# Attention's second product with its operands exchanged: the values stay in TensorE, the turned weights stream, and the division comes ahead of the turn

## The chip, the cores and the metric

The kernel runs on one core of one Trainium2 chip. The metric is the device time of one execution in microseconds, the median of several runs.

## The reference

Two transformer-like blocks are computed in fp32 on a sequence of 256 tokens of width 1024. The first block has two layers, and each layer holds a feed-forward network, a mixer and a second feed-forward network. Half of the mixer is a state-space part, the other half is an attention with 16 heads of width 64; both halves go through one output projection. The attention is a sum of three dilated causal windows whose softmax denominators are joined, which is the same as one softmax with a count for each pair of query and key. What matters here, cut down:

```python
for i in range(DEPTH):                       # 2 layers
    x = x + 0.5 * swiglu(rms_norm(x, ffn1_norm[i]), ...)
    z, xbc, dt_raw, q, k, v = split(rms_norm(x, mix_norm[i]) @ w_in[i])
    y_ssd = ssd_mixer(...)                   # (256, 1024)
    q, k = rms_norm(q, q_norm[i]), rms_norm(k, k_norm[i])
    # per head: p = exp(scores - m); den = sum(p); o = (p / den) @ v
    y_att = dilated_attention(q, k, v)       # (256, 1024)
    x = x + concatenate([y_ssd, y_att]) @ w_out[i]     # w_out: 2048 x 1024
    x = x + 0.5 * swiglu(rms_norm(x, ffn2_norm[i]), ...)
```

The second block (gated linear attention, a convolution branch, 32 experts) follows and is not touched.

## The kernel before

TensorE's order is written out by hand, and so is that of VectorE (`dve`) and ScalarE (`act`). The engines meet at semaphores. Four banks of PSUM (`misc`) are handed round: the fill with number m uses bank m % 4, TensorE waits in `claim_bank` until the fill four numbers earlier has been drained (`drained[m % 4]`), and `attention_fills()` numbers the fills of the attention: `S` for a head's scores, `T` for its turned weights and then its values, `Y` for a turn of the attended rows.

The attention of a layer is a loop over 19 steps, h = 0 to 18. It is a pipeline over heads, and the output projection is laid between its pieces:

- TensorE in step h: `scores(h)` (four instructions, lines 1211 and 1212; a plain fp32 product is two instructions), `turn_weights(h-2)` (three transposes, L1218), in steps 7, 11 and 15 also `turn_values` (four transposes, L837), `values(h-3)` (L1225), and then as many halves of rows of the output projection as `HALVES[h]` says (`out_rows`). A half is 12 instructions of 128 by 256, lines 815 to 817: the fp32 product is made of three fp32r ones, of high and low parts. The first two rows, in steps 0 and 1, are plain fp32 (L1248).
- VectorE in step h: `maxima(h)` (L2869, L2871, L2876: mask added, maximum, its scaled negative), `attended(h-3)` (L2881 the reciprocal of the sum, L2884 the values times it, from PSUM into `yatt`), in the same three steps `values_low` (L2859, low part of the turned rows), and `out_low_piece` (L2849, the low part of a row of `w_out`).
- ScalarE in step h: the exponentials of head h in two pieces with their sums (L2130, L2132), the copy of the turned weights of head h-2 out of PSUM into `pT` (L2141), `out_high_piece` (L2115, the high part of a row of `w_out`), and `values_turned` (L2124, the high part of the turned rows).

In `values(h)` a head's turned weights are the loaded (stationary) operand, and 64 columns of v stream: three products, six instructions. The result has queries on partitions. It is scaled into `yatt`, and four times per layer 256 columns of `yatt` are turned so that the output projection finds features on partitions. After step 18 come the last `turn_values(3)`, the last half of row 13, `modulation` (L1301) and rows 14 and 15; then the second feed-forward network starts (L887).

Of the kernel before, what the change touches and what calls it, by code (L numbers as in the profile page):

```python
# [116 lines left out]
def attention_fills():  # L117

    order = []
    for h in range(HEADS + 2):  # L120
        if h < HEADS:
            order.append(("S", h))
        if h >= 2:
            order.append(("T", h - 2))
        if h in TURNS:
            order.append(("Y", TURNS[h]))
    order.append(("Y", 3))
    return {step: i for i, step in enumerate(order)}


TURNS = {7: 0, 11: 1, 15: 2}
HALVES = (2, 2, 1, 2, 1, 2, 1, 1, 2, 1, 2, 1, 2, 1, 2, 1, 2, 1, 0)
PLAIN = 2
OUT_HOME = (0, None, 2, 0, None, 2, 0, None)
# [4 lines left out]
def two_blocks(nc, d, out):  # L139
    fills = []  # L140
    slots, rows_d = [], []
    for l in range(DEPTH):
        fills += [(("mod", 2), 1), (("mod", 3), 1)] * l + [(("norm", 3 * l), 4)] * (not l)
        fills += [(("ffn", 2 * l), NF)] + [("params", 4)] * (not l)
        fills += [(("mod", 4 * l), 1)]
        fills += [(("xbc", l), 8), (("dt", l), 1), (("z", l, 0), 1), (("xt", l), 4), (("bt", l), 1),
                  (("z", l, 1), 1), (("z", l, 2), 1), (("acum", l), 1), (("z", l, 3), 1), (("cb", l), 2)]
        for j in range(8):
            fills += [(("qk", l, j), 1), (("bc", l, j), 1)]
        fills += [(("v", l, 0), 1), (("v", l, 1), 1), (("state", l), 2), (("v", l, 2), 1), (("off", l), 2),  # L150
                  (("v", l, 3), 1), (("qkt", l), 8), (("yt", l), 4), (("att", l), 2 * HEADS + 4),
                  (("mod", 4 * l + 1), 1), (("ffn", 2 * l + 1), NF)]
        slots += [(("ffn", 2 * l), NF), (("win", l), 24), (("wout", l), 8), (("ffn", 2 * l + 1), NF)]
        rows_d += [(("ffn", 2 * l), NF), (("ffn", 2 * l + 1), NF)]
# [18 lines left out]
    with ctx:  # L173
# [293 lines left out]
        ysd_ready = sem("ysd_ready")  # L467
        smax_ready = sem("smax_ready")
        p_exp = sem("p_exp")
        av_done = sem("av_done")  # L470
        pt_ready = sem("pt_ready")
        out_done = sem("out_done")
# [198 lines left out]
        def y_low_of(k):  # L671

            first_ = Y_LOW + (1 - k // KD) * SLOT + k % KD * SEQ
            return high_b[:, :, :].rearrange("p a b -> p (a b)")[:, first_:first_ + SEQ]

        def turned_q(k):

# [134 lines left out]
        def _(pe):  # L812
# [391 lines left out]
            def attention_and_out(l, a):  # L1204
# [7 lines left out]
                    pe.matmul(b[:, P:3 * P], q[:, P:SEQ], k, start=True, stop=True).then_inc(filled, 1)  # L1212

                def turn_weights(h):
                    pe.wait_ge(p_exp, HEADS * l + h + 1)
                    b = claim_bank(m0 + AF["T", h])
                    for c in range(3):
                        mm = pe.transpose(b[:, c * P:(c + 1) * P], sp3[:, h % 3, c * P:(c + 1) * P], ident)  # L1218
                    mm.then_inc(filled, 1)

                def values(h):
                    pe.wait_ge(pt_ready, HEADS * l + h + 1)
                    b = bank_of(m0 + AF["T", h])
                    for t, c, key in ((0, 0, 0), (1, 1, 0), (1, 2, 1)):
                        mm = pe.matmul(b[:, 3 * P + t * HD:3 * P + (t + 1) * HD], pT[:, h % 2, c * P:(c + 1) * P],  # L1225
                                       v[:, key, h * HD:(h + 1) * HD], start=(key == 0), stop=(key == t),
                                       skip_group_check=True)
                    mm.then_inc(av_done, 1)

                def turn_values(q):  # L1230
                    for h in range(4 * q, 4 * q + 4):
                        wait_drained(pe, m0 + AF["T", h])
                    turn(m0 + AF["Y", q] - q, yatt, [q])

                def row_in(k):
                    wait_drained(pe, m0 + AF["Y", (k - KD) // 2] if k >= KD else FILL["yt", l] + k // 2)
                    if k < PLAIN:
                        wait_slot(n0 + k // 2)
                    else:
                        pe.wait_ge(out_low_in, (2 * KD - PLAIN) * l + k - PLAIN + 1)  # L1240
# [27 lines left out]
                for h in range(HEADS + 3):  # L1268
                    if h < HEADS:
                        scores(h)  # L1270
                    if 2 <= h < HEADS + 2:
                        turn_weights(h - 2)
                    if h in TURNS:
                        turn_values(TURNS[h])
                    if h >= 3:
                        values(h - 3)
                    if h == 0:
                        pe.wait_ge(acc_free, a)
                    for k, c in itertools.islice(rows_left, HALVES[h]):
                        mm = out_rows(k, c)  # L1280
                        if k % 2 and c:
                            mm.then_inc(freed[(n0 + k // 2) % SLOTS], 1)
                turn_values(3)
                for k, c in rows_left:
                    out_rows(k, c).then_inc(freed[(n0 + k // 2) % SLOTS], 1)
                modulation(4 * l + 1)
# [532 lines left out]
        def _(act):  # L1819
# [297 lines left out]
            def attention(l):  # L2117
                m0 = FILL["att", l]
                scale = HD ** -0.5

                def values_turned(q):
                    m = m0 + AF["Y", q]
                    wait_filled(act, m)
                    act.activation(xl[:, 2 * q:2 * q + 2, :], bank_of(m).rearrange("p (a b) -> p a b", a=2),  # L2124
                                   ACT.Copy).then_inc(y_high, 1)

                for h in range(HEADS + 2):
# [7 lines left out]
                    if h >= 2:  # L2135
                        hh = h - 2
                        m = m0 + AF["T", hh]
                        wait_filled(act, m)
                        if hh >= 2:
                            act.wait_ge(av_done, HEADS * l + hh - 1)  # L2140
                        act.activation(pT[:, hh % 2, :], bank_of(m)[:, 0:3 * P], ACT.Copy).then_inc(pt_ready, 1)  # L2141
                    if h in HIGH_AT:
                        out_high_piece(l, HIGH_AT[h])
                    if h in TURNS:
                        values_turned(TURNS[h])
                values_turned(3)

            def evac(m, n, dst, src_n, func=ACT.Copy, scale=1.0):

# [288 lines left out]
        def _(dve):  # L2438
# [413 lines left out]
            def attention(l):  # L2852
                m0 = FILL["att", l]

                def values_low(q):
                    dve.wait_ge(y_high, 7 * l + 3 + q + 1)
                    m = m0 + AF["Y", q]
                    first_ = Y_LOW + 2 * q * SEQ
                    dve.tensor_tensor(high_b[:, :, :].rearrange("p a b -> p (a b)")[:, first_:first_ + 2 * SEQ], bank_of(m),  # L2859
                                      xl[:, 2 * q:2 * q + 2, :].rearrange("p a b -> p (a b)").bitcast(F32), ALU.subtract)\  # L2860
                        .then_inc(drained[m % 4], 1)

                def maxima(h):
                    m = m0 + AF["S", h]
# [11 lines left out]
                    dve.tensor_scalar(nmx[:, 2 * h:2 * h + 2], mx[:, 2 * h:2 * h + 2], -(HD ** -0.5), None,  # L2876
                                      ALU.mult).then_inc(smax_ready, 1)

                def attended(h):
                    dve.wait_ge(p_exp, HEADS * l + h + 1)  # L2880
                    link(dve.reciprocal(rden[:, 2 * h:2 * h + 2], den[:, 2 * h:2 * h + 2]))  # L2881
                    dve.wait_ge(av_done, HEADS * l + h + 1)
                    m = m0 + AF["T", h]
                    dve.tensor_tensor(yatt[:, :, h * HD:(h + 1) * HD],  # L2884
                                      bank_of(m)[:, 3 * P:4 * P].rearrange("p (t e) -> p t e", t=NT),
                                      rden[:, 2 * h:2 * h + 2].unsqueeze(2).to_broadcast([P, NT, HD]), ALU.mult)\
                        .then_inc(drained[m % 4], 1)

                for h in range(HEADS + 3):
                    if h < HEADS:  # L2890
                        maxima(h)
                    if h >= 3:
                        attended(h - 3)
                    if h in TURNS:
                        values_low(TURNS[h])
                    if h in LOW_AT:
                        out_low_piece(l, LOW_AT[h])
                values_low(3)

            def modulation(p):  # L2900
                m = FILL["mod", p]
# [526 lines left out]
            for l in range(DEPTH):  # L3428
# [10 lines left out]
                    modulation(0)  # L3439
                ssd_and_projections(l)  # L3440
                for q in range(1, 4):
                    dve.wait_ge(y_high, 7 * l + q)
# [71 lines left out]
```

## Time and profile before

| what | value |
|---|---|
| median of 3 runs | 2089.66 us (2089.42 to 2098.31) |
| profiled execution, its own time | 2090.49 us |
| its span, first to last instruction | 2088.6 us |
| attention loop, layer 0 | 368.05 to 436.05 us |
| attention loop, layer 1 | 987.63 to 1055.64 us |

The loop is counted from the first instruction of `scores(0)` to the first instruction of the half row that follows the last `turn_values`. Both layers take 68.0 us, 136 us of the span together. Durations of TensorE instructions overlap, because matmuls are pipelined: what one of them costs is the distance from its start to the start of the next.

### The profile page before, as it was taken

The page shows a single profiled execution, that of the slowest core. Times are in us where ns is not written, and L with a number is a line of the kernel's source. Part 1 is how long each engine was busy: PE and PEld are TensorE (multiplying, and loading weights), DVE is VectorE, ACT ScalarE, POOL GpSimd, SP SyncE. Part 2 cuts the span into 40 slices and gives each one's busy share as a digit, 9 for nine tenths or more (in the row PEclk, how much of TensorE's full clock was granted, in tenths as well). Part 3 has the DMA queues.
Part 4 walks back from the last instruction along what each step waited for, and adds up shares of the span by engine and source line. Part 5 has one row for each costly group of instructions (what it writes and reads, how often), then busy time and mean ns, then how long its engine had stood idle before and what let it go on. Part 6 is the DMA issues. An engine that isn't in the chain of part 4 may idle for free. (4 is left out here: it accounts for less than half of the span.)

```text
span 2088.6 us, 37979 instructions
## 1 busy us (share of the span) xinstructions
PE 2049.4 (98%) x14933; PEld 1896.7 (91%) x14933; DVE 1689.3 (81%) x2097; ACT 1224.8 (59%) x1537; POOL 472.4 (23%) x253
## 2 busy tenths in 40 slices
PE   8999999999999999999999999999999999999997
PEld 8999999999999999999999998999877777777775
DVE  5887868667777877868677756998689999999998
ACT  5435565653335335666653335444378888888886
POOL 4894000008932981000009900000000000000000
PEclk9999999999999999999999999999999999999999
DMA  8875554257766774554247853445569999999994
GB/s 252 282 257 175 168 158 160 82 172 247 256 212 201 252 253 160 164 162 139 102 164 262 272 176 104 134 134 192 217 250 373 365 372 368 373 366 374 364 369 182
DMA packets 238942, 483.74 MB, mean 232 GB/s; under 512 B 10613, under 2 KB 178977, under 8 KB 222465
## 3 DMA queue, kind: packets, MB, share of 16 engines
q1 hardware_dynamic: 226880, 443.58, 60.6%
q0 software_dynamic: 11360, 37.21, 5.4%
q10 hardware_dynamic: 608, 1.65, 0.2%
q8 instruction: 65, 1.06, 0.2%
q14 instruction: 29, 0.23, 0.0%
HBM read 481.31 MB, written 1.09 MB: 231 GB/s over the span
## 5 line engine op out<-in xcount | busy, mean ns | idle before, releaser
L816 PE MATMUL misc<-xhl,ring_low 128*128 128x256 f32 x1568 | 436.5, 278 | 0.0
L815 PE MATMUL misc<-xhl,high_b 128*128 128x256 f32 x1376 | 384.1, 279 | 1.0 <-ACT xnT L1951 1.0
L817 PE MATMUL misc<-xhl,high_b 128*128 128x256 f32 x1376 | 382.8, 278 | 0.0
L816 PEld LDWEIGHTS misc<-xhl,ring_low 128*128 128x128 f32 x1568 | 295.0, 188 | 0.8
L3258 DVE TENSOR_TENSOR ring_low<-ring,high_b 128x2048 fp32r<-128x2048 f32 x128 | 287.1, 2285 | 0.6 <-issue 0.6
L2526 DVE TENSOR_TENSOR ring_low<-ring,high_b 128x2048 fp32r<-128x2048 f32 x92 | 262.8, 2894 | 10.1 <-ACT high_b L1894 9.7
L815 PEld LDWEIGHTS misc<-xhl,high_b 128*128 128x128 f32 x1376 | 260.0, 189 | 2.3 <-ACT xnT L1951 1.2
L817 PEld LDWEIGHTS misc<-xhl,high_b 128*128 128x128 f32 x1376 | 258.6, 188 | 0.0
L2253 ACT ACTIVATE high_b<-ring 128x2048 fp32r<-128x2048 f32 x124 | 235.7, 1914 | 33.7 <-DMA ring<-in_w_dram 33.2
L1794 POOL TENSOR_SCALAR arena<-arena,cact 128x1024 f32<-128x1024 f32 x56 | 213.0, 3803 | 4.9 <-DMA arena<-in_w_ada_dram 1.9
L1926 ACT ACTIVATE misc<-arena 128x256 f32<-128x256 f32 x66 | 25.7, 389 | 309.0 <-DVE arena L2574 309.0
L1550 PE MATMUL misc<-high_b,u_rows 128*128 128x512 f32 x512 | 204.1, 399 | 1.9 <-DVE u_rows L3301 1.2
L1552 PE MATMUL misc<-ring_low,u_rows 128*128 128x512 f32 x512 | 199.9, 391 | 0.0
L1894 ACT ACTIVATE high_b<-ring 128x2048 fp32r<-128x2048 f32 x92 | 170.9, 1904 | 3.1 <-DMA ring<-in_ffn_w_up_dram 3.1
L1791 POOL TENSOR_SCALAR arena<-arena,cact 128x1024 f32<-128x1024 f32 x4 | 14.5, 3618 | 615.8 <-DVE hidhl L2553 607.9
L815 PE MATMUL acc<-hidhl,high_r 128*128 128x256 f32 x528 | 148.3, 281 | 0.9 <-DVE ring_d_low L2532 0.7
L3264 DVE TENSOR_TENSOR ring_d_low<-ring_d,high_r 128x1024 fp32r<-128x1024 f32 x128 | 147.9, 1215 | 0.5
L817 PE MATMUL acc<-hidhl,high_r 128*128 128x256 f32 x528 | 147.3, 279 | 0.0
L816 PE MATMUL acc<-hidhl,ring_d_low 128*128 128x256 f32 x528 | 147.3, 279 | 0.0
L815 PE MATMUL misc<-ring_low,xhl 128*128 128x256 f32 x512 | 145.2, 284 | 1.7 <-DVE arena L2746 1.7
L2258 ACT ACTIVATE high_r<-ring_d 128x1024 fp32r<-128x1024 f32 x128 | 129.2, 1052 | 9.1 <-DMA ring_d<-in_w_dram 8.5
L1550 PEld LDWEIGHTS misc<-high_b,u_rows 128*128 128x128 f32 x512 | 96.0, 188 | 35.5 <-DVE ring_low L3258 11.0
(492 smaller groups left out, 5556.9 us busy)
## 6 DMA issues: line engine op xcount, KB each, us to landing
ring<-in_w_dram SPq DMA_DIRECT2D x128, 1024.0 KB, 7.8
ring<-in_w_in_dram SPq DMA_DIRECT2D x72, 1024.0 KB, 5.4
ring_d<-in_w_dram SPq DMA_DIRECT2D x128, 512.0 KB, 4.8
ring<-in_ffn_w_gate_dram SPq DMA_DIRECT2D x44, 1024.0 KB, 5.4
ring<-in_ffn_w_up_dram SPq DMA_DIRECT2D x44, 1024.0 KB, 9.1
ring_d<-in_ffn_w_down_dram SPq DMA_DIRECT2D x88, 512.0 KB, 7.2
arena<-in_w_ada_dram POOLq DMA_DIRECT2D x48, 512.0 KB, 5.1
ring<-in_w_out_dram SPq DMA_DIRECT2D x20, 1024.0 KB, 4.9
```

The costliest lines, as they stand in the source:

```text
L815: pe.matmul(dst, wh, ml, start=start, stop=False, **kw)
L816: pe.matmul(dst, wl, mh, start=False, stop=False, **kw)
L817: return pe.matmul(dst, wh, mh, start=False, stop=stop, **kw)
L1550: pe.matmul(b, ue[:, k, half, :], expert_part(high_b, x)[:, kk, :], start=(k == 0), stop=False)
L1552: mm = pe.matmul(b, ue[:, k, half, :], expert_part(ring_low, x)[:, kk, :], start=False, stop=(k == KD - 1))
L1794: pool.tensor_scalar(row, row, cact[:, k:k + 1], None, ALU.mult).then_inc(pool_step, 1)
L1894: act.activation(high_b[:, s, :], ring[:, s, :], ACT.Copy).then_inc(high_in[s], 1)
L2253: act.activation(high_b[:, s, :], ring[:, s, :], ACT.Copy).then_inc(high_in[s], 1)
L2258: act.activation(high_r[:, s, :], ring_d[:, s, :], ACT.Copy).then_inc(high_in_d[s], 1)
L2526: dve.tensor_tensor(ring_low[:, s, :], ring[:, s, :], high_b[:, s, :].bitcast(F32), ALU.subtract)\
L3258: dve.tensor_tensor(ring_low[:, s, :], ring[:, s, :], high_b[:, s, :].bitcast(F32), ALU.subtract)\
L3264: dve.tensor_tensor(ring_d_low[:, s, :], ring_d[:, s, :], high_r[:, s, :].bitcast(F32), ALU.subtract).then_inc(low_in_d[s], 1)
```

## The change

`values(h)` is written the other way round: 128 columns of v (the pair of heads that h belongs to) are loaded and the head's turned weights stream, 256 columns for the first 128 keys and 128 columns for the second. The result has features on partitions, and only the 64 partitions of head h are used. It lands in columns 0 to 255 of the head's own `T` bank, where the turned weights were. Because queries are now along the free axis, the division by the sum is made earlier: VectorE's `weighted(h-1)` in step h takes the reciprocal and multiplies the weights in place (128 and 256 columns), and `turn_weights` waits for it (`p_scaled`) and no longer for the exponentials. `yatt` and its turns are gone. The high and low parts are now made for each head, on 64 partitions of 256 columns: ScalarE's `values_out(h-3)` at the end of step h, ahead of `out_high_piece`, and VectorE's `values_low(h-3)`, which waits for it, ahead of `out_low_piece`. The `T` bank is drained by `values_low`. Rows 8 to 15 of the output projection wait for their two heads' banks.

```diff
-        if h in TURNS:
-            order.append(("Y", TURNS[h]))
-    order.append(("Y", 3))
...
                 def turn_weights(h):
-                    pe.wait_ge(p_exp, HEADS * l + h + 1)
+                    pe.wait_ge(p_scaled, HEADS * l + h + 1)
...
                 def values(h):
                     pe.wait_ge(pt_ready, HEADS * l + h + 1)
                     b = bank_of(m0 + AF["T", h])
-                    for t, c, key in ((0, 0, 0), (1, 1, 0), (1, 2, 1)):
-                        mm = pe.matmul(b[:, 3 * P + t * HD:3 * P + (t + 1) * HD], pT[:, h % 2, c * P:(c + 1) * P],
-                                       v[:, key, h * HD:(h + 1) * HD], start=(key == 0), stop=(key == t),
-                                       skip_group_check=True)
-                    mm.then_inc(av_done, 1)
-                def turn_values(q):
-                    for h in range(4 * q, 4 * q + 4):
-                        wait_drained(pe, m0 + AF["T", h])
-                    turn(m0 + AF["Y", q] - q, yatt, [q])
+                    ks = slice(h // 2 * P, (h // 2 + 1) * P)
+                    pe.matmul(b[:, 0:SEQ], v[:, 0, ks], pT[:, h % 2, 0:SEQ], start=True, stop=False, skip_group_check=True)
+                    pe.matmul(b[:, P:SEQ], v[:, 1, ks], pT[:, h % 2, SEQ:3 * P], start=False, stop=True,
+                              skip_group_check=True).then_inc(av_done, 1)
...
                 def row_in(k):
-                    wait_drained(pe, m0 + AF["Y", (k - KD) // 2] if k >= KD else FILL["yt", l] + k // 2)
+                    if k < KD:
+                        wait_drained(pe, FILL["yt", l] + k // 2)
+                    else:
+                        for h in range(2 * (k - KD), 2 * (k - KD) + 2):
+                            wait_drained(pe, m0 + AF["T", h])
...
-                if h in TURNS:
-                    turn_values(TURNS[h])
-                turn_values(3)
...
-                def values_turned(q):
-                    wait_filled(act, m)
-                    act.activation(xl[:, 2 * q:2 * q + 2, :], bank_of(m).rearrange("p (a b) -> p a b", a=2),
+                def values_out(h):
+                    act.wait_ge(av_done, HEADS * l + h + 1)
+                    act.activation(y_high_of(KD + h // 2)[half_of(h), :], bank_of(m0 + AF["T", h])[half_of(h), 0:SEQ],
                                    ACT.Copy).then_inc(y_high, 1)
...
                         act.activation(pT[:, hh % 2, :], bank_of(m)[:, 0:3 * P], ACT.Copy).then_inc(pt_ready, 1)
+                    if h >= 3:
+                        values_out(h - 3)
                     if h in HIGH_AT:
                         out_high_piece(l, HIGH_AT[h])
-                    if h in TURNS:
-                        values_turned(TURNS[h])
...
+                def values_low(h):
+                    dve.wait_ge(y_high, 19 * l + 3 + h + 1)
+                    m = m0 + AF["T", h]
+                    k = KD + h // 2
+                    dve.tensor_tensor(y_low_of(k)[half_of(h), :], bank_of(m)[half_of(h), 0:SEQ],
+                                      y_high_of(k)[half_of(h), :].bitcast(F32), ALU.subtract).then_inc(drained[m % 4], 1)
...
-                def attended(h):
+                def weighted(h):
                     dve.wait_ge(p_exp, HEADS * l + h + 1)
                     link(dve.reciprocal(rden[:, 2 * h:2 * h + 2], den[:, 2 * h:2 * h + 2]))
-                    dve.wait_ge(av_done, HEADS * l + h + 1)
-                    m = m0 + AF["T", h]
-                    dve.tensor_tensor(yatt[:, :, h * HD:(h + 1) * HD], ...
+                    for t, cs in ((0, slice(0, P)), (1, slice(P, 3 * P))):
+                        ins = dve.tensor_scalar(sp3[:, h % 3, cs], sp3[:, h % 3, cs], rden[:, 2 * h + t:2 * h + t + 1],
+                                                None, ALU.mult)
+                    ins.then_inc(p_scaled, 1)
...
                     if h < HEADS:
                         maxima(h)
+                    if 1 <= h <= HEADS:
+                        weighted(h - 1)
                     if h >= 3:
-                        attended(h - 3)
-                    if h in TURNS:
-                        values_low(TURNS[h])
+                        values_low(h - 3)
                     if h in LOW_AT:
                         out_low_piece(l, LOW_AT[h])
-                values_low(3)
```

## Rows read from the trace of the kernel before

**Rows 1.** The page: busy time of each engine over the span.
```profile
PE 2049.4 (98%) x14933; PEld 1896.7 (91%) x14933; DVE 1689.3 (81%) x2097; ACT 1224.8 (59%) x1537; POOL 472.4 (23%) x253
```

**Rows 2.** Busy time of each engine by stretch, attention loop of layer 0.
```profile
core 0: us, PE busy (x) PEld busy (x) DVE busy (x) ACT busy (x) POOL busy (x), PEclk, DMA share, GB/s
378.70:428.00 49.30, 49.30 (x412) 48.00 (x410) 29.27 (x105) 31.15 (x83) 0.00 (x0) 1.00 0.29 105
428.00:436.10 8.10, 7.45 (x67) 7.34 (x65) 2.91 (x8) 1.05 (x3) 0.00 (x0) 1.00 0.75 259
```

**Rows 3.** Waits between 366 and 440 us, longest first.
```profile
engine line waited for: us in total, times, longest us
ACT arena L2130 <- DVE arena L2876: 21.1, 14, 3.1
DVE arena L2869 <- PE misc L1212: 15.9, 12, 2.1
```

**Rows 4.** Timeline of TensorE, starts of steps 3, 4 and 9 to 10.
```profile
378.67 0.39 PE L1211 MATMUL misc<-arena 128*128 128x128 f32 x2
...
383.17 0.39 PE L1211 MATMUL misc<-arena 128*128 128x128 f32 x2
...
401.57 0.38 PE L1211 MATMUL misc<-arena 128*128 128x128 f32 x2
401.79 0.60 PE L1212 MATMUL misc<-arena 128*128 128x256 f32 x2
402.22 0.49 PE L1218 MATMUL misc<-konst,arena 128*128 128x128 f32 x3
402.55 0.78 PE L1225 MATMUL misc<-arena 128*128 128x64 f32 x6
403.14 0.37 PE L815 MATMUL acc<-high_b,ring_d_low 128*128 128x256 f32 x1
...
404.60 0.38 PE L1211 MATMUL misc<-arena 128*128 128x128 f32 x2
```

**Rows 5.** Timeline of TensorE, the end of the loop.
```profile
428.00 0.49 PE L1218 MATMUL misc<-konst,arena 128*128 128x128 f32 x3
...
434.24 0.78 PE L1225 MATMUL misc<-arena 128*128 128x64 f32 x6
435.67 0.63 PE L837 MATMUL misc<-konst,arena 128*128 128x128 f32 x4 [0.66 <-DVE arena L2884]
436.05 0.36 PE L815 MATMUL acc<-high_b,ring_d_low 128*128 128x256 f32 x1
```

**Rows 6.** Timeline of VectorE, around steps 8 and 9.
```profile
398.24 0.69 DVE L2859 TENSOR_TENSOR high_b<-misc,xhl 128x512 fp32r<-128x512 f32 x1 [1.97 <-ACT xhl L2124]
398.85 1.22 DVE L2849 TENSOR_TENSOR ring_low<-ring,in_z 128x1024 fp32r<-128x1024 f32 x1
399.98 0.28 DVE L2869 CUSTOM_DVE_ANT_0 arena<-misc,konst 128x128 f32<-128x128 f32 x1
...
402.43 0.29 DVE L2869 CUSTOM_DVE_ANT_0 arena<-misc,konst 128x128 f32<-128x128 f32 x1
...
435.12 0.29 DVE L2884 TENSOR_TENSOR arena<-misc,arena 128x128 f32<-128x128 f32 x1 [1.72 <-PE misc L1225]
```

**Rows 7.** Timeline of ScalarE, around steps 7 and 9.
```profile
397.63 0.58 ACT L2124 ACTIVATE xhl<-misc 128x512 fp32r<-128x512 f32 x1
...
403.31 0.40 ACT L2130 ACTIVATE arena<-arena 128x128 f32<-128x128 f32 x1
...
404.20 0.47 ACT L2141 ACTIVATE arena<-misc 128x384 f32<-128x384 f32 x1
404.57 1.04 ACT L2115 ACTIVATE ring_d_low<-ring 128x1024 fp32r<-128x1024 f32 x1
```

**Rows 8.** Groups by line and shape: busy us, mean ns | idle before.
```profile
L3301 DVE TENSOR_TENSOR u_rows<-misc,u_rows 128x256 fp32r<-128x256 f32 x68 | 25.7, 415 | 3.5 <-ACT u_rows L2290 3.4
L2290 ACT ACTIVATE u_rows<-misc 128x256 fp32r<-128x256 f32 x68 | 24.2, 378 | 22.1 <-PE misc L1538 22.1
L2998 DVE TENSOR_SCALAR arena<-arena,colc,colb 128x256 f32<-128x256 f32 x4 | 1.4, 408 | 0.2 <-DVE arena L3015 0.2
```

More of the change, by code:

```diff
@@ L124, in attention_fills @@
             order.append(("T", h - 2))
-        if h in TURNS:
-            order.append(("Y", TURNS[h]))
-    order.append(("Y", 3))
     return {step: i for i, step in enumerate(order)}
-TURNS = {7: 0, 11: 1, 15: 2}
 HALVES = (2, 2, 1, 2, 1, 2, 1, 1, 2, 1, 2, 1, 2, 1, 2, 1, 2, 1, 0)
@@ L150, in two_blocks @@
         fills += [(("v", l, 0), 1), (("v", l, 1), 1), (("state", l), 2), (("v", l, 2), 1), (("off", l), 2),
-                  (("v", l, 3), 1), (("qkt", l), 8), (("yt", l), 4), (("att", l), 2 * HEADS + 4),
+                  (("v", l, 3), 1), (("qkt", l), 8), (("yt", l), 4), (("att", l), 2 * HEADS),
                   (("mod", 4 * l + 1), 1), (("ffn", 2 * l + 1), NF)]
@@ L469, in two_blocks @@
         p_exp = sem("p_exp")
+        p_scaled = sem("p_scaled")
         av_done = sem("av_done")
@@ L674, in y_low_of, with half_of @@
             return high_b[:, :, :].rearrange("p a b -> p (a b)")[:, first_:first_ + SEQ]
+        def half_of(h):
+            return slice(h % 2 * HD, (h % 2 + 1) * HD)
         def turned_q(k):
@@ L2119, in attention @@
                 scale = HD ** -0.5
-                def values_turned(q):
-                    m = m0 + AF["Y", q]
-                    wait_filled(act, m)
-                    act.activation(xl[:, 2 * q:2 * q + 2, :], bank_of(m).rearrange("p (a b) -> p a b", a=2),
+                def values_out(h):
+                    act.wait_ge(av_done, HEADS * l + h + 1)
+                    act.activation(y_high_of(KD + h // 2)[half_of(h), :], bank_of(m0 + AF["T", h])[half_of(h), 0:SEQ],
                                    ACT.Copy).then_inc(y_high, 1)
-                for h in range(HEADS + 2):
+                for h in range(HEADS + 3):
                     if h < HEADS:
@@ L2134, in attention @@
                                        accum_out=den[:, 2 * h + 1:2 * h + 2]).then_inc(p_exp, 1)
-                    if h >= 2:
+                    if 2 <= h < HEADS + 2:
                         hh = h - 2
@@ L2141, in attention @@
                         act.activation(pT[:, hh % 2, :], bank_of(m)[:, 0:3 * P], ACT.Copy).then_inc(pt_ready, 1)
+                    if h >= 3:
+                        values_out(h - 3)
                     if h in HIGH_AT:
                         out_high_piece(l, HIGH_AT[h])
-                    if h in TURNS:
-                        values_turned(TURNS[h])
-                values_turned(3)
             def evac(m, n, dst, src_n, func=ACT.Copy, scale=1.0):
@@ L2853, in attention @@
                 m0 = FILL["att", l]
[L2855 to L2861, printed above, removed]
+                def values_low(h):
[4 more added lines that the diff above has]
+                                      y_high_of(k)[half_of(h), :].bitcast(F32), ALU.subtract).then_inc(drained[m % 4], 1)
                 def maxima(h):
@@ L2877, in maxima @@
                                       ALU.mult).then_inc(smax_ready, 1)
-                def attended(h):
+                def weighted(h):
                     dve.wait_ge(p_exp, HEADS * l + h + 1)
                     link(dve.reciprocal(rden[:, 2 * h:2 * h + 2], den[:, 2 * h:2 * h + 2]))
-                    dve.wait_ge(av_done, HEADS * l + h + 1)
-                    m = m0 + AF["T", h]
[L2884 to L2887, printed above, removed]
+                    for t, cs in ((0, slice(0, P)), (1, slice(P, 3 * P))):
+                        ins = dve.tensor_scalar(sp3[:, h % 3, cs], sp3[:, h % 3, cs], rden[:, 2 * h + t:2 * h + t + 1],
+                                                None, ALU.mult)
+                    ins.then_inc(p_scaled, 1)
                 for h in range(HEADS + 3):
@@ L3441, in _ @@
                 for q in range(1, 4):
-                    dve.wait_ge(y_high, 7 * l + q)
+                    dve.wait_ge(y_high, 19 * l + q)
                     m = FILL["yt", l] + q
```

## Prediction

> **What bounds the kernel now.** The first view is the page's list of busy time: TensorE is busy for 98% of the span [rows 1]. So I ask of every edit whether TensorE issues less, and then whether anybody makes it wait. The second view is the busy time by stretch over the attention loop, the only place that the change touches: TensorE busy for all of 49.3 us in steps 3 to 15, VectorE for 29.3, ScalarE for 31.2, the granted clock at 1.00, which is the 2.4 GHz level [rows 2]. The third is the list of waits: ScalarE waits 21.1 us for VectorE's maxima and VectorE 15.9 us for TensorE's scores [rows 3]. Both side engines follow TensorE with some slack. The reader should see how much: the slack of VectorE is 49.3 - 29.3 = 20.0 us over 13 steps, 1.5 us a step. The last views are the timelines, for the distances from start to start.
>
> **TensorE's own work.** In step 9 the scores take 401.57 to 402.22, 0.65 us; three transposes 0.33; the values 402.55 to 403.14, 0.59; one half row with its start 403.14 to 404.60, 1.46. Step 3, with two halves, takes 4.50 [rows 4]. I use 1.38 for a half (12 instructions, 0.115 apart) and 0.08 once a step that has halves.
>
> Removed: three turns in steps 7, 11, 15 and the one at the end. Four transposes at 0.11 are 0.44 each; the last costs from the end of the values to 436.05. Its values start at 434.24 and would give way to the next work 0.59 later, at 434.83, so the last turn with its wait costs 1.22 [rows 5]. Together 3 x 0.44 + 1.22 = 2.5 us a layer.
>
> Added: the values become four instructions. A plain fp32 instruction with 256 streamed columns takes 0.215 (401.79 to 402.22 is two of them), one with 128 takes 0.11 (401.57 to 401.79 is two) [rows 4]. So the new values cost 2 x 0.215 + 2 x 0.11 = 0.65 where six took 0.59: +0.06 a head, 16 heads +1.0 us a layer. The streamed columns double from 192 to 384, but the old instructions, 64 columns each, already cost 0.098 apiece. TensorE alone thus gains about 1.5 us a layer; the step-by-step count below puts it at 2.0, since it uses the rounded pieces and not each measured step. I keep 2.0 as the generous end.
>
> The Trainium skill, TensorE: Matmul & The Clock Gate, section LDWEIGHTS, says that a weight load takes its columns divided by 1.2 in ns whatever the depth, so 107 ns for 128 columns. Six loads would make the old values 0.64 us, and the exchange would be free, 1.0 us a layer better than by the rows. The trace shows 0.59, the measured distance, and the sum goes by that.
>
> **What the other engines get.** VectorE loses `attended`'s product (0.29) and a quarter of a `values_low` on 512 columns; it gains two multiplications of 128 and 256 columns and a subtraction of 256 columns per head. The multiplications have no row of this size in the loop. Bounds: the 128 by 2 instruction below, nearly nothing beyond the reciprocal; above, the 256-column TENSOR_SCALAR of L2998 at 0.41 [rows 8] twice, 0.82. With the reciprocal I take 0.75 and keep 0.2 to 1.0. It does not enter the sum, because of where it stands: between `maxima(h)` and a wait that is longer, which comes now.
>
> **The new ring.** In step h, VectorE's `values_low(h-3)` waits for ScalarE's `values_out(h-3)`. ScalarE gets to that only after the exponentials of head h, which wait for VectorE's `maxima(h)` of the same step, and after the copy to `pT`. Behind the waiting `values_low` are queued `out_low_piece` and `maxima(h+1)`. So there is a ring of VectorE and ScalarE that TensorE is no part of. Its length: `maxima` start to the first exponential, 402.43 to 403.31, 0.88 [rows 6, 7]. Both exponentials, 403.31 to 404.20, 0.89; the copy to `pT`, 404.20 to 404.57, 0.37 [rows 7]. `values_out`, 256 columns out of PSUM, as L2290, 0.38 [rows 8], and 0.03 of hand-over, as from 397.63 + 0.58 to 398.24 [rows 6, 7]. `values_low` 0.42 as L3301 [rows 8], less the 0.08 by which the next VectorE instruction starts early (398.24 + 0.69 against 398.85), 0.34. `out_low_piece` 398.85 to 399.98, 1.13 [rows 6]. The sum is 4.02; I compute with 4.01, and 2.88 in step 11, whose low piece is missing. Half the partitions are used, and I take no saving for that; were both new per-head instructions free, the ring would be 3.3, the lower bound.
>
> The wait of VectorE within it is 0.89 + 0.37 + 0.41 plus about 0.05, 1.7 us after `maxima`. The division, 0.75, hides in it, and would only enter if it took over 1.7.
>
> TensorE needs 0.65 + 0.33 + 0.65 + 1.46 = 3.09 us for a step with one half and 4.47 with two. The 13 steps 3 to 15 hold 19 halves: 13 x (1.63 + 0.08) + 19 x 1.38 = 48.5. The ring needs 12 x 4.01 + 2.88 = 51.0. The ring is the slower by 2.5 us, so TensorE will wait.
>
> **Where it waits.** `turn_weights(h-2)` claims the bank that `values_low(h-4)` drains in VectorE's step h-1. That drain is usable to TensorE 0.88 + 0.89 + 0.37 + 0.41 + 0.42 after the start of that step's `maxima`, plus 0.26, as from 435.12 + 0.29 to 435.67 [rows 5, 6]: 3.23. I carry two lines from step 3 on. `maxima(h)` starts at the later of TensorE's step start + 0.86 (scores out) and the previous `maxima` + 4.01; the turn in step h starts at the later of step start + 0.65 and the previous `maxima` + 3.23. From 378.67 [rows 4] and a first `maxima` at 379.70 the step starts come out as 383.14, 386.23, 391.05, 394.14, 397.69, 403.08, 406.17, 411.10, 414.19, 419.12, 422.21, 427.03, 430.12, 435.05, 437.49, and the end of the loop at 438.14. Waits stand in steps 5 (0.35), 7 (0.46), 8 (0.92), 10 (0.46), 12 (0.46), 14 (0.35) and 16 (1.11), 4.1 us in all. Step 16 has the longest, because no scores stand ahead of the turn and the lag is exposed. The loop is then 438.14 - 368.05 = 70.1 us instead of 68.0: 4.1 of waits less 2.0 of work, +2.1 a layer. Steps 0 to 2 have no `values_low` and stay.
>
> Behind the loop nothing absorbs it: the half row, `modulation` and rows 14 and 15 are TensorE's own, and the drains of heads 12 to 15 come under the half row (1.4) and `modulation`. Two layers: +4.2 us. Against the profiled execution, 2088.6 of span and 2090.49 in all, that is 2092.8 and 2094.7; the median of the runs shown is 0.8 lower, so 2093.9.
>
> **Rivals.** First, TensorE stays the bound. If the ring is 3.6 us or less, for instance because the instructions on 64 partitions are short, only waits of 1.3 us a layer are left; with none at all both layers gain 4.1: 2085.6. For it speaks the slack of 1.5 us a step; against it that the ring's terms are measured rows, and that ScalarE's part of it was no part of VectorE's order before. Chance 0.09.
>
> Second, slower: the ring is 4.5. One mechanism, the hand-overs within the ring: `values_out` behind a wait on TensorE's values and `values_low` behind ScalarE. Each 0.1 of ring costs about 2.2 us over both layers, 12 steps each. At 4.5 it is +15, 2104.6. It decides from a ring of 4.3, where it is +10.3. For it: in a chain of four dependent pieces a small extra counts every time. Against: the hand-overs are in the rows. Chance 0.10.
>
> Third, the ring exists but is partly absorbed: the loop's waits overlap with the starts of half rows, or the next stage takes the lateness up. Half of +4.2, 2091.8. The two layers' loops were alike to 0.01 us, which speaks against any slack behind them. Chance 0.17.
>
> **Numbers.** My forecast has 0.64: 2093.9. A step of 0.5%, 10.4 us, is about what a measurement tells from no change. The range reaches from 2087.5 (a ring of 3.6 gives 2088.3 by the same two lines, the edge to the first rival) to 2101.5 (a ring of 4.35 gives 2101.2), and leaves out the first two rivals, 0.19. Faster by over 0.5% would need 5.2 us a layer; TensorE gives back 2.0 at most: 0.02, for what I don't see. Slower by over 0.5% is the second rival and a little: 0.11. The rest, 0.87, is within.
>
> **What would show it.** Right: L1225 gone to four instructions of 128x256 and 128x128, 0.65 a head; no L837 in the loop; VectorE's subtraction waits about 1 us for ScalarE each step, after a division of 0.75; from one `maxima` to the next 4.0 us from step 5 on, however many halves TensorE has; TensorE idle ahead of L1218, longest in step 16; each loop 70.1 us. Wrong: steps of 3.1 and 4.5 in turn without idle time would be the first rival; 4.3 or more between maxima the second.

## The result and the profile after

The changed kernel takes 2092.76 us (median of 20 runs, 2082.84 to 2105.91), the kernel before in the same comparison 2087.73 (20 runs): the medians lie 5.0 us apart. The ratio that the comparison of the runs gives is 1.003, 95% interval 1.0015 to 1.0044, or +6.3 us (3.1 to 9.2). Timed once more beside an experiment below, it was 1.0035 (1.0019 to 1.0051); one of those ten runs took 2907 us at a granted clock of 0.65, a slower state, and is left out. Slower, but by less than the 0.5% that I had set as the bound of no change.

The page of the changed kernel, its span and its busy times:

```profile
span 2085.3 us, 37821 instructions
...
PE 2038.2 (98%) x14837; PEld 1880.7 (90%) x14837; DVE 1706.5 (82%) x2153; ACT 1233.6 (59%) x1561; POOL 480.0 (23%) x253
```

This is the first trap. The profiled execution of the slower kernel has a span of 2085.3 us, 3.3 less than that of the kernel before, and its line of busy times looks like [rows 1]. One execution says nothing of a difference of 0.3%: other stages scatter by more. The attention loop scatters by about 0.1 us; it can be measured from mark to mark, from the first instruction of `scores(0)` to the half row behind the loop. In the profile of the changed kernel that is 369.49 to 440.88 us, 71.4, and 71.35 in the second layer, where before had 68.0 twice.

Busy time by stretch, the same window as the first of [rows 2] (columns as there):

```profile
core 0: us, PE busy (x) PEld busy (x) DVE busy (x) ACT busy (x) POOL busy (x), PEclk, DMA share, GB/s
378.70:428.00 49.30, 44.94 (x342) 41.40 (x341) 34.51 (x121) 31.28 (x82) 0.00 (x0) 1.00 0.32 108
```

TensorE was busy for all of these 49.3 us before and is now idle for 4.4 of them; the granted clock is still 1.00. Who is waited for, in the waits from 366 to 440 us:

```profile
engine line waited for: us in total, times, longest us
ACT arena L2125 <- DVE arena L2869: 22.0, 16, 2.6
DVE high_b L2853 <- ACT xhl L2119: 17.5, 14, 2.3
...
PE misc L1219 <- DVE high_b L2853: 4.4, 6, 1.2
DVE arena L2862 <- PE misc L1213: 3.9, 4, 1.6
```

Three lines are to be read against [rows 3]. VectorE's wait for TensorE's scores (here L2862 on L1213) fell from 15.9 to 3.9 us: in most steps VectorE no longer follows TensorE. It waits 17.5 us for ScalarE's `values_out` instead, 14 times, 1.2 us as a rule. And there is a line that before did not have: TensorE's turn (L1219) waits for `values_low` (L2853), 4.4 us. Step 8 on TensorE's timeline has the largest of these waits:

```profile
399.62 0.38 PE L1212 MATMUL misc<-arena 128*128 128x128 f32 x2
399.84 0.60 PE L1213 MATMUL misc<-arena 128*128 128x256 f32 x2
401.61 0.52 PE L1219 MATMUL misc<-konst,arena 128*128 128x128 f32 x3 [1.17 <-DVE high_b L2853]
401.97 0.60 PE L1226 MATMUL misc<-arena 128*128 128x256 f32 x2
402.40 0.38 PE L1227 MATMUL misc<-arena 128*128 128x128 f32 x2
402.54 0.36 PE L816 MATMUL acc<-high_b,ring_d_low 128*128 128x256 f32 x1
...
405.37 0.38 PE L1212 MATMUL misc<-arena 128*128 128x128 f32 x2
```

The scores end 0.65 after the start of the step, at 400.27; the turn starts at 401.61. The new values are four instructions and take 401.97 to 402.54. The step is 5.75 us long, where step 8 before was 4.39, 397.18 to 401.57.

The ring itself, two turns of it. VectorE's timeline, steps 7 and 8 (the reading of the accumulators left out):

```profile
398.37 0.29 DVE L2862 CUSTOM_DVE_ANT_0 arena<-misc,konst 128x128 f32<-128x128 f32 x1
...
399.32 0.55 DVE L2876 TENSOR_SCALAR arena<-arena 128x128 f32<-128x128 f32 x2
401.05 0.42 DVE L2853 TENSOR_TENSOR high_b<-misc,xhl 64x256 fp32r<-64x256 f32 x1 [1.18 <-ACT xhl L2119]
401.39 1.21 DVE L2843 TENSOR_TENSOR ring_low<-ring,in_z 128x1024 fp32r<-128x1024 f32 x1
402.52 0.28 DVE L2862 CUSTOM_DVE_ANT_0 arena<-misc,konst 128x128 f32<-128x128 f32 x1
...
405.19 0.43 DVE L2853 TENSOR_TENSOR high_b<-misc,xhl 64x256 fp32r<-64x256 f32 x1 [1.19 <-ACT xhl L2119]
405.65 1.23 DVE L2843 TENSOR_TENSOR ring_low<-ring,in_z 128x1024 fp32r<-128x1024 f32 x1
406.91 0.29 DVE L2862 CUSTOM_DVE_ANT_0 arena<-misc,konst 128x128 f32<-128x128 f32 x1
```

And ScalarE's, the same two steps:

```profile
399.25 0.40 ACT L2125 ACTIVATE arena<-arena 128x128 f32<-128x128 f32 x1 [1.55 <-DVE arena L2869]
...
400.26 0.49 ACT L2136 ACTIVATE arena<-misc 128x384 f32<-128x384 f32 x1
400.65 0.36 ACT L2119 ACTIVATE xhl<-misc 64x256 fp32r<-64x256 f32 x1
...
403.39 0.40 ACT L2125 ACTIVATE arena<-arena 128x128 f32<-128x128 f32 x1 [1.43 <-DVE arena L2869]
...
404.28 0.47 ACT L2136 ACTIVATE arena<-misc 128x384 f32<-128x384 f32 x1
404.78 0.38 ACT L2119 ACTIVATE xhl<-misc 64x256 fp32r<-64x256 f32 x1
```

The reader should follow it round once: maxima (L2862) 398.37, exponentials 399.25, copy to `pT` 400.26, `values_out` 400.65, `values_low` 401.05, low piece 401.39, maxima 402.52: 4.15 us. The next round, 402.52 to 406.91, takes 4.39. The two alternate from the maxima of step 4 to those of step 11, and again at the end of the loop, 4.27 on average, in both layers, however long TensorE's step is. In between, step 11 has no low piece and takes 3.02, and step 12 takes 4.92, because its next maxima wait for TensorE. The division (L2876, both multiplications 0.55) lies inside VectorE's wait.

### The profile page after: what moved, and what is told of

It reads as the page before. It is cut to its first block and busy times, and to the rows that moved or that the text cites. A ratio compares the mean times of both kernels' runs of the same rounds, so it can differ in the third digit from the quotient of the medians.

```text
span 2085.3 us, 37821 instructions
## 1 busy us (share of the span) xinstructions
PE 2038.2 (98%) x14837; PEld 1880.7 (90%) x14837; DVE 1706.5 (82%) x2153; ACT 1233.6 (59%) x1561; POOL 480.0 (23%) x253
## 5 line engine op out<-in xcount | busy, mean ns | idle before, releaser
L1790 POOL TENSOR_SCALAR arena<-arena,cact 128x1024 f32<-128x1024 f32 x56 | 219.3, 3916 | 4.4 <-DMA arena<-in_w_ada_dram 1.3
L1787 POOL TENSOR_SCALAR arena<-arena,cact 128x1024 f32<-128x1024 f32 x4 | 15.4, 3856 | 623.1 <-DVE hidhl L2547 613.9
```

The lines of the kernel that those rows point to most:

```text
L1790: pool.tensor_scalar(row, row, cact[:, k:k + 1], None, ALU.mult).then_inc(pool_step, 1)
```

## The experiments

All loops below are measured as above, layer 0 and layer 1 in one number where they agree to 0.1. The other two columns are the stretches between the two loops and behind the second, in single profiled executions.

| kernel | loop | between | behind |
|---|---|---|---|
| before, first profile | 68.0 | 551.6 | 1033.0 |
| before again | 68.0 | 552.0 | 1029.8 |
| changed, first profile | 71.4 | 546.9 | 1026.1 |
| changed again | 71.4 | 549.2 | 1034.3 |
| halves swapped | 71.0 | 550.7 | 1029.7 |
| low piece first | 67.6 | 547.0 | 1026.8 |
| no division | 71.3 | 554.5 | 1024.6 |
| full width | 68.7 | 552.2 | 1027.2 |
| `values_out` in the middle | 67.1 | 550.0 | 1029.6 |
| `values_out` first | 65.7 | 546.2 | 1028.4 |
| division alone | 68.2 | 546.6 | 1028.5 |

**The kernel before once more**, without an edit.

> The kernel before, unchanged, profiled once more. In the profile of the changed kernel both attention loops grew by 3.4 to 3.5 us, but the stretch between them was 4.7 us shorter and the one behind them 6.9 us shorter, where nothing was edited. If that is scatter of other stages, this run shows attention loops of 68.0 us again (to 0.1) while its other two stretches differ from the first profile's 551.6 and 1033.0 us by several us. If instead the change shortens the other stages, they repeat here within 1 us.

The loops are 68.01 both times. The stretch behind is 3.2 us shorter than in the first profile, the one between came back to 0.4, which is not the several us that I expected there. The table settles it: none of these kernels does other work outside the loops (only what rows 14 and 15 wait for has changed), and the stretches spread over 546 to 555 and 1025 to 1034 us, those of the changed kernel itself by 8.2. What the change does to the loops can be measured; that it also moves the rest can neither be shown nor excluded at this size.

**The multiplications left out.** The run leaves out the two multiplications and keeps the reciprocal, and not the whole division as its expectation says.

```diff
                     link(dve.reciprocal(rden[:, 2 * h:2 * h + 2], den[:, 2 * h:2 * h + 2]))
-                    for t, cs in ((0, slice(0, P)), (1, slice(P, 3 * P))):
-                        ins = dve.tensor_scalar(sp3[:, h % 3, cs], ...)
-                    ins.then_inc(p_scaled, 1)
+                    dve.nop().then_inc(p_scaled, 1)
```

> The changed kernel, leaving out the division: no reciprocal and no multiplications of the weights, only the signal. Theory: they stand inside VectorE's wait of 1.2 us for ScalarE, so that wait grows to about 2.0 us, and ring and loop stay within 0.3 us of 4.27 and 71.5. Rival: the division is what delays the turns and the low pieces; then the ring falls by 0.75 to 3.5 and the loop to about 67.

Loop 71.3 and 71.4, ring 4.15 and 4.38 as before. Waits from 364 to 441 us:

```profile
DVE high_b L2853 <- ACT xhl L2119: 27.1, 15, 2.7
```

The wait for ScalarE grew from 1.2 to 1.8 us a time, by the 0.55 of the multiplications: what VectorE does not do, it waits. They cost nothing here. The wait of 2.0 that I expected counted the reciprocal too; its 0.20 stands in the same wait but was not taken out.

**The division alone**, put into the kernel before: `weighted(h-1)` in step h, `attended` a plain copy out of PSUM, operands and turns as they were.

```diff
                 def turn_weights(h):
-                    pe.wait_ge(p_exp, HEADS * l + h + 1)
+                    pe.wait_ge(p_scaled, HEADS * l + h + 1)
...
                     if h < HEADS:
                         maxima(h)
+                    if 1 <= h <= HEADS:
+                        weighted(h - 1)
```

> The kernel before, with one part of the change alone: the division made ahead of the turn (weighted(h-1) in step h, attended a plain copy); operands and turns of the attended rows as before. Theory: VectorE had 1.5 us of slack a step and the turn is a step later, so the loop stays at 68.0 (to 0.3). Rival: the new wait of the turn for VectorE holds TensorE up; loop above 69.

Loop 68.2, 0.2 more than before, all of it in steps 8 and 9 (4.54 and 3.18 us for 4.39 and 3.03). In the changed kernel the multiplications cost nothing, in the kernel before the earlier division costs at most this 0.2 of a loss of 3.4.

**The low piece ahead of `values_low`.**

```diff
-                    if h >= 3:
-                        values_low(h - 3)
                     if h in LOW_AT:
                         out_low_piece(l, LOW_AT[h])
+                    if h >= 3:
+                        values_low(h - 3)
```

> The changed kernel, with VectorE's out_low_piece put ahead of values_low. Theory (the ring decides): the low piece, 1.13 us, falls into VectorE's wait for ScalarE, so the ring shrinks from 4.27 to 3.1 and maxima follow TensorE's steps (3.1 and 4.5 us in turn), while the drain of the T bank comes no earlier, 3.5 us after the step's maxima; TensorE waits about 0.6 in each step that follows one with a single half row, 3 us a layer instead of 5, loop 69.1 instead of 71.5. Rival (the new product or the division costs the time): loop stays at 71.5.

The profile of this run, VectorE's timeline, step 8:

```profile
399.90 0.29 DVE L2862 CUSTOM_DVE_ANT_0 arena<-misc,konst 128x128 f32<-128x128 f32 x1 [0.28 <-PE misc L1213]
...
401.31 1.22 DVE L2843 TENSOR_TENSOR ring_low<-ring,in_z 128x1024 fp32r<-128x1024 f32 x1
402.59 0.43 DVE L2853 TENSOR_TENSOR high_b<-misc,xhl 64x256 fp32r<-64x256 f32 x1
404.47 0.29 DVE L2862 CUSTOM_DVE_ANT_0 arena<-misc,konst 128x128 f32<-128x128 f32 x1 [1.45 <-PE misc L1213]
```

The same instructions in another order: the low piece fills the wait, the maxima wait for TensorE again, and the loop falls by 3.8 us to 67.6, below the kernel before. That is more than the forecast of 69.1, since the turn that waits for the drain starts 3.24 or 3.25 and not 3.5 after the maxima of the step before, and TensorE's own work is less than I had counted. What is left are waits of 0.2 to 0.3 us on the drain of the T bank in five steps.

**`values_out` between the exponentials and the copy to `pT`.**

```diff
+                    if h >= 3:
+                        values_out(h - 3)
                     if 2 <= h < HEADS + 2:
                         hh = h - 2
...
-                    if h >= 3:
-                        values_out(h - 3)
```

> The changed kernel, with values_out(h-3) between the exponentials and the copy to pT. The ring stays closed but loses one term, the copy of 0.37 to 0.49 us: 3.9 instead of 4.27 on average. By the two lines of the prediction with these numbers the loop takes 68.0 us. Rival (the ring's length is not what sets the loop): no change from 71.4, or the full gain of the version above.

The ring is 3.64 and 4.01 us, 3.83 on average, a saving of 0.44 where the copy was taken out of it, and the loop is 67.1. The loop follows the ring's length, which is the theory's point; its forecast, 68.0, was 0.9 too high. Only one wait of TensorE for the drain is left, 0.7 us in step 8.

**`values_out` first**, ahead of the exponentials of the same step.

```diff
                 for h in range(HEADS + 3):
+                    if h >= 3:
+                        values_out(h - 3)
                     if h < HEADS:
                         act.wait_ge(smax_ready, HEADS * l + h + 1)
...
-                    if h >= 3:
-                        values_out(h - 3)
```

> The changed kernel, with ScalarE's values_out(h-3) at the beginning of step h, ahead of the exponentials, so that VectorE's values_low no longer waits for this step's maxima. Theory (the ring alone costs the time): values_low starts without a wait right after the division, maxima follow TensorE's steps, the T bank is drained early enough, and TensorE waits for nobody: its own saving shows bare, loop 66.0 us where before had 68.0 and the changed kernel 71.4; in all 4 us below before (ratio 0.998) and 10.7 below the changed kernel. Rival (the product written this way is slower on TensorE than its distances say): loop no lower than 68.

2075.82 us (12 runs) against 2085.12 of before on the same chip, medians 9.3 us apart; the ratio of the comparison is 0.9963 (0.9949 to 0.9977), 7.7 us faster than before (4.8 to 10.6), where I had expected 4. It beats both kernels. Its waits from 360 to 436 us:

```profile
ACT xhl L2119 <- PE misc L1227: 18.8, 16, 2.8
DVE arena L2862 <- PE misc L1213: 12.0, 9, 1.6
DVE high_b L2853 <- ACT xhl L2119: 5.3, 3, 3.3
```

Both side engines wait for TensorE, and no line of TensorE waiting in the loop is left. VectorE's timeline shows a step without the ring; `values_low` starts right behind the division:

```profile
403.78 0.55 DVE L2876 TENSOR_SCALAR arena<-arena 128x128 f32<-128x128 f32 x2
404.37 0.43 DVE L2853 TENSOR_TENSOR high_b<-misc,xhl 64x256 fp32r<-64x256 f32 x1
404.82 1.23 DVE L2843 TENSOR_TENSOR ring_low<-ring,ring_d_low 128x1024 fp32r<-128x1024 f32 x1
407.31 0.29 DVE L2862 CUSTOM_DVE_ANT_0 arena<-misc,konst 128x128 f32<-128x128 f32 x1 [1.26 <-PE misc L1213]
```

The step on TensorE that begins at 406.45 ends at 409.51, 3.06 us, with the new values from 407.44 to 408.01. The loop is 65.74 in both layers, TensorE's work with almost no wait (0.14 is left in step 16, where the values start 0.47 after the turn instead of 0.33): 2.3 less than before a layer, and 5.6 less than the changed kernel's, which is therefore what its waits cost. The two loops explain 4.5 of the 7.7 us; the interval's near end is 4.8, and the profiles cannot say where the rest lies. The same holds against the changed kernel, 15.0 us by the medians where the loops give 11.3.

**The changed kernel timed beside it.**

> The changed kernel as it is, timed beside the version above on the same chip. Loops 71.4 us each again, 6.8 us more than before in both layers; ratio to before 1.003.

Loops 71.3 and 71.45; 2090.86 (9 runs) against 2085.12, ratio 1.0035. Two loops of +3.4 are 6.8 us, inside the interval of 4.0 to 10.6.

**The halves of the partitions swapped.** The ring was forecast at 4.01 and measured at 4.39 and 4.15 in turn. What alternates is the half of the partitions that `values_out` and `values_low` work on.

```diff
         def half_of(h):
-            return slice(h % 2 * HD, (h % 2 + 1) * HD)
+            return slice((1 - h % 2) * HD, (2 - h % 2) * HD)
```

> The changed kernel, but even heads use partitions 64 to 127 of the product and odd heads 0 to 63; it leaves out the right half of each pair of heads, so its attended values are those of the neighbour's columns, in the same amount of work. In the changed kernel the ring of VectorE and ScalarE takes 4.39 us where head h-3 is odd and 4.15 where it is even, instead of the 4.01 forecast. Theory A: the longer one belongs to partitions 64 to 127; then 4.39 comes in the steps with even h-3 and 4.15 in those with odd. Theory B: it belongs to the parity of the head (its PSUM bank, its buffer); then nothing moves.

VectorE's timeline, steps 8 and 9, whose heads are 5 and 6; only the maxima and `values_low` are shown:

```profile
397.52 0.29 DVE L2862 CUSTOM_DVE_ANT_0 arena<-misc,konst 128x128 f32<-128x128 f32 x1
...
400.20 0.42 DVE L2853 TENSOR_TENSOR high_b<-misc,xhl 64x256 fp32r<-64x256 f32 x1 [1.18 <-ACT xhl L2119]
...
401.68 0.28 DVE L2862 CUSTOM_DVE_ANT_0 arena<-misc,konst 128x128 f32<-128x128 f32 x1
...
404.34 0.43 DVE L2853 TENSOR_TENSOR high_b<-misc,xhl 64x256 fp32r<-64x256 f32 x1 [1.18 <-ACT xhl L2119]
...
406.06 0.29 DVE L2862 CUSTOM_DVE_ANT_0 arena<-misc,konst 128x128 f32<-128x128 f32 x1
```

Head 5, which took the long turn in step 8, now has the lower half and 4.16 us; head 6 has the upper half and 4.38. The long turn goes with partitions 64 to 127, and not with the head's bank or buffer.

**Both instructions on all 128 partitions**, the columns unchanged.

```diff
         def half_of(h):
-            return slice(h % 2 * HD, (h % 2 + 1) * HD)
+            return slice(0, P)
...
                 def values_out(h):
+                    if h % 2:
+                        wait_drained(act, m0 + AF["T", h - 1])
```

> The changed kernel, with values_out and values_low on all 128 partitions for every head, and a wait of values_out, for odd heads, until the head before has been drained; each head then overwrites its neighbour's half, so it leaves out half of the attended values, at the same number of columns. The run with the halves swapped showed that the ring's length follows the partitions: 4.38 where the head's half is 64 to 127, 4.15 where it is 0 to 63. Theory A: what costs is a neighbour in the queue on another range of partitions; then no step has it, and the ring is the 4.0 us of the forecast in every step, loop 69.0. Theory B: a head with an odd number costs more for another reason that happened to move with the swap; then 4.15 and 4.38 alternate on, loop 71.4.

VectorE's timeline, the turns of steps 7 and 8:

```profile
398.83 0.43 DVE L2855 TENSOR_TENSOR high_b<-misc,xhl 128x256 fp32r<-128x256 f32 x1 [1.05 <-ACT xhl L2121]
399.17 1.22 DVE L2845 TENSOR_TENSOR ring_low<-ring,in_z 128x1024 fp32r<-128x1024 f32 x1
400.30 0.28 DVE L2864 CUSTOM_DVE_ANT_0 arena<-misc,konst 128x128 f32<-128x128 f32 x1
...
402.84 0.43 DVE L2855 TENSOR_TENSOR high_b<-misc,xhl 128x256 fp32r<-128x256 f32 x1 [1.05 <-ACT xhl L2121]
```

Here 402.84 - 398.83 is 4.01, and every turn with a low piece that VectorE sets the pace of is 4.01 or 4.02: the sum of the prediction to the hundredth. The loop is 68.65. Twice the partitions cost nothing; working on the halves in turn cost 0.26 us a turn on average.

## Why the prediction was right, and where its sizes were off

**The bound and the mechanism: right.** I forecast that TensorE saves work, that a ring of VectorE and ScalarE takes the pace, and that TensorE waits for the drain of the T bank. The profile shows this wait in steps 5, 7, 8, 10, 12 and 14, where the two lines of the prediction had put it, the largest in step 8; moving instructions in or out of the ring moved the loop each time (71.4, 67.6, 67.1, 65.7), and taking the multiplications out did not. Nothing right behind the loop absorbed it, as forecast: from the end of the loop to the first product of L887 (L888 in the changed kernel) it is 9.33 us before and 9.33 after. Forecast +4.2 us in all, measured +6.3 (3.1 to 9.2); by the loops alone it is 6.8. That the median of 2092.76 lies only 1.1 from the forecast of 2093.9 is in part luck: the forecast starts from three runs of the kernel before with a median of 2089.66, and twenty runs of it gave 2087.73.

**The length of the ring: 4.01 forecast, 4.27 measured.** The step that was mis-sized is "Half the partitions are used, and I take no saving for that". There was no saving but a cost. Of the terms, maxima 0.88, exponentials 0.89, `values_out` 0.41 and `values_low` 0.34 were as forecast where the head lies in the lower half. With the upper half, `values_out` starts 0.50 after the copy and not 0.37, the low piece 0.46 after `values_low` and not 0.34, the maxima 1.26 after the low piece and not 1.13; and one turn later the copy starts 1.01 after the exponentials and not 0.89. Over a pair of heads this is 0.5 us, 0.25 a turn. At full width the loop is 68.65; the halves cost 2.7 of the changed kernel's 71.4.

**The waits: 4.1 a layer forecast, 5.6 measured** (71.4 less 65.74). The longer ring makes the waits in steps 7, 8, 10 and 12 longer: against `values_out` first, these steps take 1.0 to 1.3 us more, where I had 0.46, 0.92, 0.46 and 0.46; steps 5 and 14 take 0.3 more, as forecast. One of mine was wrong: the 1.11 in step 16. I let every turn wait for the bank of two heads earlier, but in step 16 no scores are issued, the order of the fills shifts, and `turn_weights(14)` takes the bank of `scores(14)`. TensorE's timeline of the changed kernel in step 16 shows no idle time ahead of the turn and some ahead of the values, which wait for the copy to `pT`:

```profile
433.47 0.55 PE L1219 MATMUL misc<-konst,arena 128*128 128x128 f32 x3
434.35 0.70 PE L1226 MATMUL misc<-arena 128*128 128x256 f32 x2 [0.34 <-ACT arena L2136]
```

The turn would have given way after 0.33, at 433.80; the values start 0.55 later. So the two errors, a wait too many and a ring too short, went against each other, and that the total still came near is luck. At full width, where the ring is the 4.01 of the forecast, the waits are 68.65 - 65.74 = 2.9 us, and the forecast without step 16 was 3.0: the two lines were right but for that step.

One more hit hides two errors. The waiting turn starts 3.24 or 3.25 us after the `maxima` of the step before, in all six waits, and the forecast had 3.23. In it one late start beside the upper half, of the copy to `pT` or of `values_out`, costs 0.12 that I had not counted, and from the end of `values_low` to the turn it takes 0.14 and not 0.26.

**TensorE's own work: -2.0 forecast, -2.3 measured.** A step with a turn of the attended rows gave back 0.46 net of the exchanged product (3.51 to 3.05), so the turn itself took 0.48, and 0.44 was the forecast. The exchanged product cost less: a step with one half takes 3.05 where before took 3.03, so +0.02 a head and not +0.06 (steps with two halves came out between 0.03 shorter and 0.09 longer), and its instructions stand 0.57 apart from first to next work, where the sum had 0.65. The two of 128 columns take 0.14 together (407.87 to 408.01), not the 0.22 that such a pair takes in the scores. The rule of the Trainium skill (TensorE: Matmul & The Clock Gate, section LDWEIGHTS) on weight loads, 107 ns each, would have made the exchange free. The trace comes nearer to that than my sum, though the old six instructions, which started 0.098 us apart, still lie below the rule.

**The division: nothing, as forecast.** It took 0.75 with the reciprocal (0.20 to the multiplications, 0.55 for them) and lay in the wait. The run took out the 0.55; that the 0.20 is free as well is read from its place in the same wait.

**The rivals.** TensorE staying the bound needed a ring of 3.6; out of reach here, but `values_out` first brings TensorE back as the bound, by opening the ring. The ring of 4.5, the slower rival, had the right direction of the error: hand-overs were not longer (0.03 to 0.04 each), neighbours in a queue were. Partial absorption did not occur in the loops, and behind them it is below the scatter.

## What to carry to other kernels

When a step of one engine is made to wait for another engine's work of the same turn, write down the ring that closes, with everything queued between, and compare its length with the pace of the engine that bounds; each engine can have slack by itself and the ring none. If the ring is too long, the remedy is order and not speed: here one line moved on ScalarE turned 0.3% slower into 0.4% faster, since what was waited for had been ready before the exponentials that stood ahead of it began (in step 8 the values end at 402.78 and the exponentials start at 403.39). And where a stage repeats to 0.1 us inside a program that scatters by 0.5%, measure the stage.

## What the runs showed of the hardware that was not expected

Work on 64 partitions was no faster than on 128: `values_low` 0.42 to 0.43 against 0.43 us, `values_out` 0.36 to 0.38 against 0.37. But it disturbed its neighbours when it lay on partitions 64 to 127. Instructions that otherwise start about 0.1 us before the end of the one ahead (0.37 after a copy of 0.47) then start just after that end (0.50), on ScalarE and on VectorE, at four places in a pair of turns, 0.12 us each; on partitions 0 to 63 the same instructions did it at none of them. Two of the four places stand directly beside the instruction on the upper half; the maxima behind the low piece and the copy behind the next turn's exponentials do not. A fifth place lies outside the ring: the high piece starts 0.41 after `values_out` on the upper half and 0.27 after it on the lower.

All five fit one pattern. It is a reading of these traces; no run was made to test it. An instruction loses its early start when the last instruction of its engine that read the same memory (PSUM or SBUF), or wrote to it, began at another partition. The maxima read PSUM, and the last instruction of VectorE that did so was `values_low`, at partition 64; the low piece between them reads only SBUF. The copy to `pT` reads PSUM, and the last of ScalarE to do so was `values_out` of the turn before. The runs with `values_out` moved agree. Here it stands in the middle, a head in the lower half first and then one in the upper:

```profile
397.09 0.36 ACT L2119 ACTIVATE xhl<-misc 64x256 fp32r<-64x256 f32 x1
397.35 0.47 ACT L2138 ACTIVATE arena<-misc 128x384 f32<-128x384 f32 x1
397.72 1.05 ACT L2111 ACTIVATE in_z<-ring 128x1024 fp32r<-128x1024 f32 x1
...
400.83 0.38 ACT L2119 ACTIVATE xhl<-misc 64x256 fp32r<-64x256 f32 x1
401.24 0.49 ACT L2138 ACTIVATE arena<-misc 128x384 f32<-128x384 f32 x1
401.62 1.05 ACT L2111 ACTIVATE ring_d_low<-ring 128x1024 fp32r<-128x1024 f32 x1
```

The copy, now right behind `values_out`, is late (0.41 instead of 0.26), and the high piece behind the copy no longer is (0.38 and 0.37). With `values_out` first, the exponentials behind it are late (0.40 instead of 0.28), and so is the copy behind them (0.22 instead of 0.09). The run at full width starts at partition 0, as the neighbours do, so it cannot tell the half from its start. What in the engine does it stays open.
